# Attention heads as one stream of tiles, values for four heads at once, projections in pieces between the tiles

## The reference, cut to what matters

```python
kv_up = (ckv_all @ p['kv_w_up']).reshape(B, past + L, 8, 128 + 128)
k_nope, v_all = kv_up[..., :128], kv_up[..., 128:]
q = rms_norm(hin @ p['mla_w_dq'][j], g) @ p['mla_w_uq'][j]     # per head 128 + 64
q_pe = apply_rope(q[..., 128:], cos, sin)
s = einsum(q_nope, k_nope) + einsum(q_pe, k_pe)                # then * scale
allowed = (k_pos // 64) <= (q_pos // 64)
o = einsum(softmax(where(allowed, s, -inf)), v_all)
mix = o.reshape(B, L, 1024) @ p['mla_w_out'][j]
```

## Time and profile before

| | us |
|---|---|
| median of 3 runs | 3671.08 (3669.82 to 3676.69) |
| profiled execution | 3674.14 |
| its span, first to last instruction | 3672.3 |
| mean granted TensorE clock | 0.936 |

### The profile page before, as it was taken

One profiled execution on the slowest core, in us unless ns is written; L12 is line 12 of the kernel. 1 busy time (PEld: TensorE's weight loads), 2 busy tenths in 40 slices (PEclk: granted clock), 3 DMA queues, 4 the chain that ended last, 5 costly groups with the idle time before them and its releaser, 6 DMA issues.

```text
span 3672.3 us, 52802 instructions
## 1 busy us (share of the span) xinstructions
PE 3339.1 (91%) x19861; PEld 3026.1 (82%) x19861; DVE 1863.8 (51%) x2614; ACT 1011.0 (28%) x1799; POOL 952.6 (26%) x687
## 2 busy tenths in 40 slices
PE   5999979998897999999986889999985999999996
PEld 2999979997486999999985756665684999999995
DVE  3999956664314555554556532222224455455556
ACT  1222234443204222222224422222213222212223
POOL 0322235552334222222212210000024222222222
PEclk8999989998798999999998987898897999999998
DMA  5444621111210111111111100000020111111111
GB/s 200 162 166 161 236 65 47 36 28 42 93 41 23 45 42 45 46 46 46 40 40 35 44 24 12 12 23 12 12 88 13 51 42 44 46 46 46 43 43 49
DMA packets 83444, 214.22 MB, mean 58 GB/s; under 512 B 9161, under 2 KB 40650, under 8 KB 82194
## 3 DMA queue, kind: packets, MB, share of 16 engines
q1 hardware_dynamic: 32640, 121.79, 10.4%
q10 hardware_dynamic: 50706, 91.07, 7.5%
HBM read 184.12 MB, written 28.71 MB: 58 GB/s over the span
## 4 chain that ended last, share of the span: by engine, by line
PE 77%; DVE 8%; issue 5%; POOL 4%; ACT 4%; DMA 1%; DVEq 0%; ACTq 0%; POOLq 0%; SPq 0%
PE PS L310 18%; PE PS L314 17%; PE PS L313 17%; PE PS L1653 3%; PE PS L1652 3%; PE PS L1678 2%; PE PS L563 2%; PE PS L577 2%; PE PS L1167 2%; DVE CV L2127 2%; DVE CV L2124 2%; POOL TB L478 1%; POOL SUMX L1151 1%; PE PS L1667 1%; ACT X L1188 1%
## 5 line engine op out<-in xcount | busy, mean ns | idle before, releaser
L310 PE MATMUL PS<-HH,WH 128*128 128x354 f32 (+1 forms) x3432 | 1124.4, 328 | 124.1 <-DVE HL L487 64.7
L314 PE MATMUL PS<-HH,WL 128*128 128x354 f32 (+1 forms) x3432 | 1122.0, 327 | 0.0
L313 PE MATMUL PS<-HL,WH 128*128 128x354 f32 (+1 forms) x3432 | 1121.5, 327 | 0.0
L306 POOL TENSOR_TENSOR WL<-RAW,WH 128x1024 fp32r<-128x1024 f32 x197 | 518.8, 2633 | 1385.2 <-ACT WH L301 1384.8
L310 PEld LDWEIGHTS PS<-HH,WH 128*128 128x128 f32 x3432 | 654.4, 191 | 133.1 <-issue 131.2
L313 PEld LDWEIGHTS PS<-HL,WH 128*128 128x128 f32 x3432 | 654.9, 191 | 0.2
L314 PEld LDWEIGHTS PS<-HH,WL 128*128 128x128 f32 x3432 | 652.5, 190 | 0.0
L1440 DVE SCALAR_TENSOR_TENSOR X<-PS,ADA,X 128x354 f32<-128x354 f32 x704 | 330.4, 491 | 438.8 <-PE PS L314 438.7
L310 PE MATMUL PS<-FH,WH 128*128 128x354 f32 (+1 forms) x1056 | 361.5, 342 | 22.6 <-DVE FL L1431 14.4
L301 ACT ACTIVATE WH<-RAW 128x1024 fp32r<-128x1024 f32 x197 | 209.0, 1061 | 593.6 <-PE PS L310 587.8
L313 PE MATMUL PS<-FL,WH 128*128 128x354 f32 (+1 forms) x1056 | 344.3, 326 | 0.0
(11 more groups left out here) (266 smaller groups left out, 4294.6 us busy)
## 6 DMA issues: line engine op xcount, KB each, us to landing
RAW<-ws SPq DMA_DIRECT2D x197, 512.0 KB, 3.5
ADR<-wada ACTq DMA_DIRECT2D x72, 512.0 KB, 4.7
scr<-V ACTq DMA_DIRECT2D x32, 530.0 KB, 3.5
AD<-wada SPq DMA_DIRECT2D x4, 2048.0 KB, 23.5
X<-xT SPq DMA_DIRECT2D x1, 4240.0 KB, 16.9
ZL<-scr ACTq DMA_DIRECT2D x8, 530.0 KB, 3.3
scr<-OH ACTq DMA_DIRECT2D x8, 530.0 KB, 2.8
KF<-scr ACTq DMA_DIRECT2D x8, 512.0 KB, 3.9
```

What stands on the lines that cost most here:

```text
L306: e.tensor_tensor(WL[u][:, :], RAW[:, u, :], WH[u][:, :].bitcast(fp32), ALU.subtract).then_inc(lo_done, 1)
L310: mm = e.matmul(out, WH[w][:, c:c + 128], mh, start=first, stop=False)
L313: e.matmul(out, WH[w][:, c:c + 128], ml, start=False, stop=False)
L314: return e.matmul(out, WL[w][:, c:c + 128], mh, start=False, stop=last)
```

## The change

Weights. The slabs of the heads hold only query and key weights now; two new slabs hold the value weights of heads 0 to 3 and of heads 4 to 7, 512 columns for each half of the latent. NSLAB grows by two.

Values. `pe_v` does 11 tiles of 6 matmuls with 512 moving columns each, one bank to a tile. The first batch comes ahead of the last rotation, over six banks; the second at tile 0 of head 4, with bank 7 alone. VT holds 11 x 512 columns.

Mask. The position product goes over 128 partitions: the lower 64 of QPX hold this head's positional query, copied there by POOL chunk by chunk (`pool_qpx`), the upper 64 of QPX and of KPE hold indicator rows and the mask, loaded once. The matmul on one partition is gone.

Stream. The loops are written out. Tiles are counted through, x = 9 h + t, and scores run two tiles ahead across the ends of heads. Head h + 1's key pieces stand at tiles 0 to 3 and its query pieces at tiles 3, 5 and 7 of head h, each between the transposes and the scores of the tile two on. All these pieces use bank 7, and each waits until the piece before it has been copied. KT has two buffers; QT has one, written chunk by chunk when the tiles that read it have passed. Products with values use bank 6 only. The splits of the following slab come after the exponential at tile 2.

```diff
-S_MO = S_HD + HEADS
+S_MO = S_HD + HEADS + 2
...
+        Q_AT, Q_USED = {3: 0, 5: 1, 7: 2}, (3, 6, 9)
+        def pieces_at(x):
+            h, t = divmod(x, NQ)
+            out = [("v", 1, b) for b in range(NV)] if (h, t) == (HALF, 0) else []
+            if h + 1 < HEADS:
+                out += [("k", h + 1, t)] if t < len(KCH) else []
+                out += [("q", h + 1, Q_AT[t])] if t in Q_AT else []
+            return out
+            P_BANK[p_] = n_ % 6 if n_ < len(P_FIRST) else 7
+            P_PREV[p_] = at_bank.get(P_BANK[p_])
+        def pe_v(e, B, b):
...
+            if P_PREV[p]:
+                evacuated(e, P_PREV[p])
+            out = PS[:, P_BANK[p], :]
+            for k in range(LB):
+                c = slice(512 * k, 512 * k + 512)
+                mm = e.matmul(out, CKH[:, k, c0:c0 + 128], WH[w][:, c], start=(k == 0), stop=False)
...
+                e.matmul(out, CKH[:, k, c0:c0 + 128], WL[w][:, c], start=False, stop=False)
+                mm = e.matmul(out, CKL[:, k, c0:c0 + 128], WH[w][:, c], start=False, stop=(k == LB - 1))
+            mm.then_inc(pj_ps, 1)
+        def pe_score(e, x):
...
+                e.matmul(out, QT[:, q0:q0 + P], KT[h % 2][:, k0 + s0_:k0 + s0_ + w_], start=True, stop=False)
+                mm = e.matmul(out, QPX[:, q0:q0 + P], KPE[:, k0 + s0_:k0 + s0_ + w_], start=False, stop=True)
+            mm.then_inc(sc_ps, 1)
...
+            for x in range(NX):
+                h, t = divmod(x, NQ)
+                pe_weights(e, x)
+                if (h, t) == (HALF, 0):
+                    for b in range(NV):
+                        pe_v(e, 1, b)
+                if h + 1 < HEADS and t < len(KCH):
+                    pe_k(e, h + 1, t)
+                if h + 1 < HEADS and t in Q_AT:
+                    pe_q(e, h + 1, Q_AT[t])
+                if x + 2 < NX:
+                    pe_score(e, x + 2)
+                pe_ov(e, x)
...
+        def act_heads(a):
...
+                act_pt(a, x)
+                if (h, t) == (HALF, 0):
+                    for b in range(NV):
+                        act_v(a, 1, b)
+                        if b == 0:
+                            split_hi(a, slab_h(HALF + 1), slab_h(HALF + 1) % 2)
+                if h + 1 < HEADS and t in Q_AT:
+                    act_q(a, h + 1, Q_AT[t])
+                if x + 2 < NX:
+                    act_exp(a, x + 2)
+                if t == 2 and h + 1 < HEADS:
+                    n = slab_v(1) if h == HALF - 1 else slab_h(h + 2) if h + 2 < HEADS else S_MO
+                    split_hi(a, n, n % 2)
+                act_ov(a, x)
...
+        def vec_heads(v):
...
+                if x + 1 < NX:
+                    vec_normalise(v, x + 1)
                 if t in BIG:
...
+                    v.wait_ge(pu_ps, nbig(x) + 1)
+                    past(v, ov_ps, x)
                     nb = len(key_blocks(t)) - 4
                     v.tensor_copy(PT[:, 4:4 + nb, :], bank(5)[:, 0:nb, :]).then_inc(pu_ev, 1)
+                if h + 1 < HEADS and t < len(KCH):
+                    vec_k(v, h + 1, t)
+                if x + 2 < NX:
+                    vec_top(v, x + 2)
+        def pool_heads(p):
...
+            for h in range(HEADS - 1):
+                if h == HALF:
+                    split_lo(p, slab_h(h + 1), slab_h(h + 1) % 2)
+                n = slab_v(1) if h == HALF - 1 else slab_h(h + 2) if h + 2 < HEADS else S_MO
+                split_lo(p, n, n % 2)
+                for ch in range(NCH):
+                    pool_qpx(p, h + 1, ch, n)
...
             rope(2)
+            all_here(e, (lh_rdy, 4), (ll_rdy, 4), (up_ev, 3 * G_MO))
+            for b in range(NV):
+                pe_v(e, 0, b)
             rope(3)
-            with e.Fori(0, HEADS // 2) as i:
-                for u in range(2):
-                    pe_head(e, i, u)
-            all_here(e, (ov_ev, NQ * HEADS))
+            pe_heads(e)
+            e.wait_ge(ov_ev, NX)
...
             pool_cos(p, 3)
+            split_lo(p, slab_h(0), slab_h(0) % 2)
```

More of the change, by code:

```diff
@@ L1606, in key_blocks @@
             return [(first + m, min(128, nk - 128 * m)) for m in range(-(-nk // 128))]
-        def scores(t):
-            q0, P, k0, nk = QTILES[t]
[L1610 to L1669, removed]
-                if t in BIG:
[L1671 to L1711, removed]
-                ins.then_inc(pt_ev, 1)
-                if t + 2 < NQ:
-                    weights(t + 2)
-                all_here(a, (ov_ps, NQ * h + t + 1))
-                if t == 0:
-                    all_here(a, (o_st[u], 16 * i))
-                a.activation(OH[u][:, q0:q0 + P], PS[:, 6 + t % 2, 0:P], ACT.Copy).then_inc(ov_ev, 1)
-            all_here(a, (ov_ev, NQ * h + NQ))
-            a.dma_start(scr[ds(h, 1), :, :].rearrange("a p n -> p (a n)"), OH[u][:, :]).then_inc(o_st[u], 16)
@@ new lines, in pe_k @@
+        def pe_k(e, h, ch):
+            p = ("k", h, ch)
+            n, (c0, cw) = slab_h(h), KCH[ch]
+            if ch == 0:
+                all_here(e, (hi_done, n + 1), (lo_done, n + 1))
+            if P_PREV[p]:
+                evacuated(e, P_PREV[p])
+            for k in range(LB):
+                mm = three(e, PS[:, P_BANK[p], 0:cw], n % 2, 128 * (QB + k), CKH[:, k, c0:c0 + cw], CKL[:, k, c0:c0 + cw], k == 0, k == LB - 1,
+                           ch == 0 and k == 0)
+            mm.then_inc(pj_ps, 1)
@@ new lines, in pe_weights @@
+        def pe_weights(e, x):
+            t = x % NQ
+            q0, P, k0, nk = QTILES[t]
+            e.wait_ge(nm_rdy, x + 1)
+            past(e, pt_ev, x)
+            past(e, pu_ev, nbig(x))
+            blocks = key_blocks(t)
+            for m, (b, kw) in enumerate(blocks):
+                mm = e.transpose(PS[0:kw, 4 + m // 4, (m % 4) * 128:(m % 4) * 128 + P], PR[x % 2][0:P, 128 * m:128 * m + kw], con(C_ID, P, P))
+                if m == min(4, len(blocks)) - 1:
+                    mm.then_inc(pt_ps, 1)
+            if t in BIG:
+                mm.then_inc(pu_ps, 1)
@@ new lines, in pe_ov @@
+        def pe_ov(e, x):
+            h, t = divmod(x, NQ)
+            P = QTILES[t][1]
+            evacuated(e, ("v", h // HALF, NV - 1))
+            e.wait_ge(pt_ev, x + 1)
+            past(e, pu_ev, nbig(x + 1))
+            past(e, ov_ev, x)
+            blocks = key_blocks(t)
+            c = 128 * (h % HALF)
+            for m, (b, kw) in enumerate(blocks):
+                mm = e.matmul(PS[:, 6, 0:P], VT[0:kw, b, c:c + 128], PT[0:kw, m, 0:P], start=(m == 0), stop=(m == len(blocks) - 1))
+            mm.then_inc(ov_ps, 1)
@@ new lines, in act_q, with act_v, act_exp @@
+        def act_q(a, h, ch):
+            c0, cw = CHS[ch]
+            a.wait_ge(pj_ps, P_DONE["q", h, ch])
+            past(a, sc_ps, NQ * (h - 1) + Q_USED[ch])
+            a.activation(QT[:, c0:c0 + cw], PS[:, P_BANK["q", h, ch], 0:cw], ACT.Copy).then_inc(qv_ev, 1)
+        def act_v(a, B, b):
+            a.wait_ge(pj_ps, P_DONE["v", B, b])
+            past(a, ov_ps, NQ * HALF * B)
+            a.activation(VT[:, b, :], PS[:, P_BANK["v", B, b], :], ACT.Copy).then_inc(qv_ev, 1)
+        def act_exp(a, x):
+            t = x % NQ
+            q0, P, k0, nk = QTILES[t]
+            a.wait_ge(mx_rdy, 2 * x + 2)
+            past(a, pt_ps, x - 1)
+            past(a, pu_ps, nbig(x - 1) if x else 0)
+            a.activation(PR[x % 2][0:P, 0:nk], scores(x), ACT.Exp, scale=SCALE, bias=SMX[0:P, 1, t:t + 1],
+                         accum_out=SMX[0:P, 2, t:t + 1]).then_inc(ex_rdy, 1)
@@ new lines, in act_pt @@
+        def act_pt(a, x):
+            t = x % NQ
+            P = QTILES[t][1]
+            a.wait_ge(pt_ps, x + 1)
+            past(a, ov_ps, x)
+            full = [m for m, (b, kw) in enumerate(key_blocks(t)) if kw == 128 and m < 4]
+            rest = [(m, kw) for m, (b, kw) in enumerate(key_blocks(t)) if kw < 128]
+            ins = a.activation(PT[:, 0:len(full), 0:P], bank(4, 128, P)[:, 0:len(full), :], ACT.Copy)
+            for m, kw in rest:
+                ins = a.activation(PT[0:kw, m, 0:P], PS[0:kw, 4, m * 128:m * 128 + P], ACT.Copy)
+            ins.then_inc(pt_ev, 1)
@@ L1906, in pool_rest @@
                 ins = p.memset(OH[u][:, SEQ:SAM], 0.0)
-            with p.Fori(0, HEADS // 2) as i:
-                for u in range(2):
-                    pool_head(p, i, u)
+            pool_heads(p)
             pool_split_run(p, S_MO + 1, KB)
@@ L1939, in vec_rest @@
                     vec_rope(v, b + 1, ch, QPE[:, b, :], OH0)
-            with v.Fori(0, HEADS // 2) as i:
-                for u in range(2):
-                    vec_head(v, i, u)
+            vec_heads(v)
             for ch, (c0, cw) in enumerate(CHS):
```

190 lines of the change are left out of this document (138 added, 52 removed).

## The result

| | before | after |
|---|---|---|
| median of the runs, us | 3673.89 | 3511.12 |
| span of the profiled execution, us | 3672.3 | 3509.1 |
| first score of head 0 to the last values, us | 513.7 | 347.2 |
| first score of head 0, from the span's start | 2148.3 | 2151.2 |
| mean granted clock | 0.936 | 0.954 |

The change makes the kernel faster, 0.9557 of the time before (95% interval 0.954 to 0.9574). The runs of before that the ratio uses have a median of 3673.89, 2.8 us above the one that the forecast started from.

What follows compares the result with a forecast made beforehand. The prediction took TensorE, busy for nearly the whole span, as the bound. Its terms, 32.8 + 26.9 + 18.1 - 10.2 - 1.9 + 50 = 116 us, took 3674.1 to 3558, or 3555 as median of runs; range 3530 to 3604.

Steps and rivals of the forecast that it cites:

- The position product grows from 64 to 128 partitions; I cost that at nothing.: Attention scores: widening the position product costs TensorE nothing, since matmuls on 1 and 128 partitions were each busy 0.48 us.
- The clock: Attention tiles: falls to 1.2 GHz cost 61 us in all; two falls, 11 us, remain; gain 50 us.
- Values: Value matmuls: 512 columns cost 0.231 us each; 56.9 us go, a second batch of 24.1 stays; gain 32.8 us.
- Rival (d): Value batches: wide matmuls cost 0.5 us each, 18 us more per batch, the first partly covered: 3591 us; chance 0.05.
- Mask: Scores: 64 mask matmuls on one partition, 0.42 us each, go; gain 26.9 us.
- Waits: Tiles and head ends: TensorE's waits for DVE and ACT shrink by 7.7, 4.9 and 5.5 us; gain 18.1 us.
- The new wait: Tile 3: first query piece waits 1.45 us for DVE's copy of the last key piece, in seven heads; loss 10.2 us.
- The entry: Before head 0: key pieces wait for POOL's subtraction, first score at about 2150.2; loss 1.9 us.
- (a): Attention tiles: the clock falls at every head as before, so the 50 us gain goes: 3605 us; chance 0.17.
- (e): Attention stage: the clock never recovers and the stage runs at 1.2 GHz, slower at 3814 us; chance 0.03.
- (b): Attention stage: no clock fall worth telling and DVE early enough at tile 3, 11 + 10 us more: 3534; chance 0.12.
- (c): Tiles: POOL's subtractions hold DVE up, 2.15 us each, nine in the stage, 19 us: 3574 us; chance 0.08.

## Why the forecast was wrong, step by step

- **"The position product grows from 64 to 128 partitions; I cost that at nothing."** This step failed, and it is the larger part of the error: 38 us of gain, by the run on 64 partitions. I bounded a loss and took none; a gain I did not bound. Its ground was that busy times on 1 and 128 partitions were equal, 0.48 us each. Both stood beside a 64-partition product, so the equality only said that both paid. What the runs showed in place of the nothing: a weight load in the open for each 64-partition product and for its neighbour, 0.42 us a step where 0.22 do. The sign was in the trace: in the earlier trace rows the step of 128 columns was 0.42 and that of 512 columns 0.96, four times the columns for 2.3 times the step. So some 0.24 us of each step did not go by columns ((4 x 0.42 - 0.96) / 3), and I never asked what they were.
- **The clock** was right in that the falls go and mis-sized, 62 for 50, because I left two falls: at head 0 and in the second batch. There were none, though PE waits 0.7 us after each 1.7 us in that batch. The reason I gave, the narrow values and their wait, does not hold: with both kept and no product on few partitions 16 slow us were left, and with the values cut to a sixth the falls stayed. That the term came near is luck in part. Few-partition matmuls matter in the kernel before (144 slow us with them, 16 without), yet alone in the stream they brought 0 and 8; what makes the clock fall stays open.
- **Values**: matmuls of 512 columns step by 0.23 us (starts at 2341.95 and 2342.18) as drawn from 354 and 256; the batch cost 25.9 for 24.1. The first batch is covered, as told. Rival (d) is out.
- **Mask**: 29 us between the runs with and without, 26.9 forecast.
- **Waits**: 14.8 for 18.1. The wait at tile 6 grew from 0.8 to 1.2 us, as cheaper scores cover less of DVE's chain (0.9 in the run on 64 partitions); the failed step reaches here too.
- **The new wait** was right: 1.34 us, seven times, 1.45 forecast, and moving the piece removed it.
- **The entry** was right: 2151.2 for 2150.2, with the last rotation, POOL's two instructions and PE's 5.0 us in that order.
- **Rivals.** (a) and (e) are out: no fall. (b) named the clock rightly at 3534 but kept the wait at tile 3 out and had no word for the steps. (c), POOL holding DVE up: once it did, at the entry, where DVE's addition took 2.65 us beside the subtraction. Moving the subtraction gained 8.3 us, but most of that was PE's own wait of 5.0 us for its result and the slow projections behind it. Inside the tiles nothing was held up: DVE's copies, maxima and normalisations have the mean durations that they had before, within 0.03 us.

The timeline of PE at the entry and at tile 3, after:

```profile
2139.24 0.64 PE L313 MATMUL PS<-CKH,WH 128*128 128x354 f32 x1 [4.96 <-issue]
2151.15 0.46 PE L1705 MATMUL PS<-KT,QT 128*128 128x128 f32 x2 [0.96 <-ACT QT L1765]
...
2207.88 0.43 PE L313 MATMUL PS<-QLH,WH 128*128 128x354 f32 x1 [1.34 <-DVE KT L1831]
```

## What to carry to other kernels

Price a matmul by the distance between starts and set it against its columns at the granted clock; where much of it is unexplained, ask what stands beside it, and bound an edit that changes a shape on the side of gain too. Where a product needs half of the partitions, the free half can carry a mask at no cost to PE, and the loads of its neighbours are covered again. When PE stands at a wait between pieces of filler work, place the pieces where the list of waits has its entries, and not two on one bank in a row.

## What the runs showed of the hardware that I had not expected

- A product on 64 partitions between products on 128 costs itself 0.2 us and its neighbour 0.1 to 0.2, 34 us over 104 such pairs; on 96 partitions nothing. In the records shown, the weight load for the 64-partition product does not begin ahead of its matmul.
- The clock fell to 1.2 GHz in the heads of the kernel before, where PE never waited longer than 1.1 us, and stayed at 2.4 GHz in the second batch of values, with ten waits of 0.7 us. Taking out the matmuls on one partition removed some three fifths of the slow time, moving values and projections without touching them nearly all.
- Two parts of a change can each remove the same slow clock: 112 and 97 us alone, 163 together.
